# Value products of the attention stage: turned for the local heads, one per head instead of one per map for the differential heads

## The chip, the cores and the metric

One NeuronCore of a Trainium2 chip runs the whole kernel. Its engines are TensorE (PE; PEld is its weight load), VectorE (DVE), ScalarE (ACT), GpSimd (POOL) and SyncE (SP). The metric is the time of one execution on the device, in microseconds; the rows below come from one profiled execution.

## The reference

Two transformer blocks run on 256 tokens of width 1024, all in f32. The change lies in the attention of the second block, between its input projection and its output projection. This is what is computed there:

```python
# 8 local heads (SWA) on 2 key/value heads: window of 128, a sink, 64 wide
scores = einsum("bnqhgd,bnkhd->bnhgqk", qb, kk) * HEAD_DIM ** -0.5 - slope * dist   # masked
p = softmax(concatenate([scores, sink], axis=-1))[..., :-1]
out = einsum("bnhgqk,bnkhd->bnqhgd", p, vv)          # then rms_norm over all 512 columns
# 4 differential heads: two maps each, one value head of 128
p = softmax(s)                                       # s: (b, h, 2 maps, q, k), causal
p_diff = p[:, :, 0] - lam * p[:, :, 1]
out = einsum("bhqk,bkhe->bqhe", p_diff, v)           # then rms_norm over each head's 128
```

Both outputs side by side, 1024 columns, are multiplied with `w_out`.

## The kernel before, in words

Activations lie feature by token (128 features on the partitions, 256 tokens along the row). A large product is made three times in f32r, high and low parts of weight and activation (`products`, L1852 to L1854). Weights stream through a ring of four units: ScalarE rounds a unit to `w_hi`, VectorE (in this stage) makes `w_lo`, three units ahead of use.

The second block's input projection `in2` has 18 units, its output projection `out2` 8. The attention is threaded between them in numbered steps, one unit per step in steps 0 to 17, written out by hand in `make_steps`; each engine has one loop over `STEPS` and does in each step, in a fixed order, what the step's entries say. An engine takes its instructions in order, so one that waits holds up all behind it. Nothing is planned at run time.

There are 16 maps of softmax scores (`MAPS`): 0 to 7 are the local heads, 8 to 15 the two maps of each differential head. Map m goes through these steps:

- step m+3 (a pair of maps at once, every second step): TensorE's `score_pair` (L2125), four f32 products on halves of the array, 64 rows each; VectorE's `biased_max` (L1627, L1634): bias and mask, then two maxima; ScalarE's `exps` (L1063) with row sums.
- step m+4: TensorE's `transposes` (L2145) of the three 128x128 pieces of probabilities into `probT_ps`; ScalarE's `copy_prob_T` (L1071); VectorE's `denominators` (L1640, L1645).
- step m+5: TensorE's `value_product` (L2160 to L2163), three f32 products with the transposed probabilities as weights and V as the moving operand (64 columns wide for a local head, 128 for a differential one) into `pv_ps`; VectorE's `scaled_output` (L1654, L1661, L1665) divides by the denominators and adds the second map to the first.

When all local heads (i = 0) or both maps of a differential head (i = 1 to 4) are there, ScalarE squares and sums (`y_squares`, L1080), VectorE makes the mean square (`y_mean_square`, L1670), GpSimd raises it to -1/2 (L714), VectorE scales (`y_scaled`, L1677). TensorE transposes 128 columns of the result, a chunk (`y_transposes`, L2178); VectorE applies the gain (`y_gained`, L1688, L1691), ScalarE rounds (`round_chunk`, L817), VectorE makes the rest (`rest_of_chunk`, L1234). There are 8 chunks, 0 to 3 local, 4 to 7 differential, and `out2` multiplies each with 8 units of weights.

Step 18 and later have no projection unit; there `out2_part(i, first, end)` begins unit i with the chunks that are there. One step, LATE_STEP, does its chunk after the scores and not before; up to it `y_scaled` stands behind `biased_max` on VectorE, and from it on ahead. VectorE's order in a step is: mean square, copies out of the projection (`copy_out`, L1613), gains, denominators, scaled output, (late scaling), rests of chunks, bias and maxima, (scaling), `w_lo` (L1168).

Of the kernel before, what the change touches and what calls it, by code (L numbers as in the profile page):

```python
# [20 lines left out]
P = 128  # L21
# [65 lines left out]
N_MAPS, N_SWA = 16, 8  # L87

# [7 lines left out]
LATE_STEP = 16  # L96
# [5 lines left out]
def make_steps():  # L102
    steps = [dict(unit=u if u < len(IN2_TILES) else None, copies=[], v_trans=None, pair=None,
                  score=None, trans=None, pv=None, y_sum=None, y_scale=None, y_chunks=[], out2=None)
             for u in range(23)]
# [9 lines left out]
    for i in range(5):  # L115
        at = (7 if i == 0 else 7 + 2 * i) + 5
        steps[at]["y_sum"], steps[at + 1]["y_scale"] = i, i
        steps[at + 2]["y_chunks"] = [0, 1] if i == 0 else [3 + i]
        if i == 0:
            steps[at + 3]["y_chunks"] = [2, 3]  # L120
    there = 0
    for n, step in enumerate(steps):
        if 0 <= n - len(IN2_TILES) < OUT2_BEGUN:
            step["out2"] = (n - len(IN2_TILES), there)
        there += len(step["y_chunks"])
# [6 lines left out]
for _step in STEPS:  # L132
# [4 lines left out]
    _tiles += _y_tiles + _v_tiles  # L137
# [102 lines left out]
def tile_release():  # L240
# [21 lines left out]
    for tile, t in IN2_TILE.items():  # L262
        r[t] = ("src_ready", CHUNK0["y"] + tile[1] + (2 if tile[1] < 4 else 1)) if tile[0] == "y" else \
            ("v_ready", tile[1] + 1) if tile[0] == "v_T" else ("copied", COPIED[tile])
# [6 lines left out]
def build(nc, d):  # L271
# [4 lines left out]
    with ExitStack() as ctx:  # L276
# [102 lines left out]
        y_a, y_b = place("y_a", [P, 2, 512]), place("y_b", [P, 2, 512])  # L379
# [14 lines left out]
        def y_tile(c):  # L394
# [4 lines left out]
            return bank[IN2_TILE["y", c - half] % RING][:, half * TOK:(half + 1) * TOK]  # L399

# [111 lines left out]
        yT_done = sem("yT_done")  # L512
        post_gain_in = sem("post_gain_in")
# [98 lines left out]
        def _(pool):  # L612
# [80 lines left out]
            for c in range(DC):  # L693
# [5 lines left out]
                if c > 0:  # L699
# [9 lines left out]
                                    ).then_inc(rstd_ready, 1)  # L709
            for n, step in enumerate(STEPS):  # L710
                if step["y_scale"] is not None:
                    i = step["y_scale"]
                    pool.wait_ge(y_ms_done, i + 1)
                    nc.gpsimd.tensor_tensor(y_rstd[:, i, :], y_ms[:, i, :], minus_half[:, 0:2],  # L714
                                            ALU.pow).then_inc(y_rstd_done, 1)
                if 0 < n <= len(IN2_TILES):
                    rest_of_unit(UNIT0["in2"] + n + LEAD)
# [45 lines left out]
        def _(act):  # L763
# [309 lines left out]

            def y_squares(i):
                act.wait_ge(y_done, 2 * (8 if i == 0 else 8 + 2 * i))
                for b in range(2):
                    part = y_a[:, b, :] if i == 0 else y_b[:, b, P * (i - 1):P * i]
                    if 2 * i + b:
                        act.wait_ge(y_ss_done, 2 * i + b)
# [4 lines left out]
            for n, step in enumerate(STEPS):  # L1084
                for c in step["y_chunks"] if n != LATE_STEP else []:
# [7 lines left out]
                if step["v_trans"] is not None:  # L1093
                    copy_v(step["v_trans"])
                if step["trans"] is not None:
                    copy_prob_T(step["trans"])
                if 3 <= n < len(IN2_TILES) + len(OUT2_SIDE):
# [30 lines left out]
            act.wait_ge(y_ss_done, 10)  # L1128
# [31 lines left out]
        def _(dve):  # L1160
# [476 lines left out]
            def denominators(m):  # L1637
                kind, h, part = MAPS[m]
                dve.wait_ge(exp_done, 2 * (m + 1))
                nc.vector.reciprocal(rden[:, m, :], row_sum[:, m, :]).then_inc(den_done, 1)  # L1640
# [7 lines left out]
            def scaled_output(m):  # L1648
                kind, h, part = MAPS[m]
                dve.wait_ge(pv_done, m + 1)  # L1650
                dve.wait_ge(den_done, DEN[m])
                for b in range(2):
                    if kind == "swa":
                        nc.vector.tensor_scalar(y_a[:, b, HD * h:HD * (h + 1)],  # L1654
                                                pv_ps[:, HD * b:HD * (b + 1)],
                                                rden[:, m, b:b + 1], None, ALU.mult
                                                ).then_inc(y_done, 1)
                    else:
                        y, pv = y_b[:, b, P * h:P * (h + 1)], pv_ps[:, P * b:P * (b + 1)]
                        if part == 0:  # L1660
                            nc.vector.tensor_scalar(y, pv, rden[:, m, b:b + 1], None, ALU.mult  # L1661
                                                    ).then_inc(y_done, 1)
                        else:
                            dve.wait_ge(y_done, 2 * m)
                            nc.vector.scalar_tensor_tensor(y, pv, rden[:, m, b:b + 1], y, ALU.mult,  # L1665
                                                           ALU.add).then_inc(y_done, 1)

            def y_mean_square(i):
                dve.wait_ge(y_ss_done, 2 * (i + 1))
                nc.vector.tensor_scalar(y_ms[:, i, :], y_ss[:, i, :], 1.0 / (512 if i == 0 else P),  # L1670
                                        EPS, ALU.mult, ALU.add).then_inc(y_ms_done, 1)

            def y_scaled(i):
                dve.wait_ge(y_rstd_done, i + 1)
                for b in range(2):
                    y = y_a[:, b, :] if i == 0 else y_b[:, b, P * (i - 1):P * i]
                    nc.vector.tensor_scalar(y, y, y_rstd[:, i, b:b + 1], None, ALU.mult  # L1677
                                            ).then_inc(y_norm, 1)

            def y_gained(c):  # L1680
# [3 lines left out]
                dve.wait_ge(yT_done, (c // 2 * 2 + 2) if c < 4 else c + 1)  # L1684
                src_free(n)
                source = y_tile(c)
                if c < 4:
# [720 lines left out]
```

## Time and profile before

| | us |
|---|---|
| median of 3 runs | 759.88 (759.86 to 760.01) |
| profiled execution | 760.85 |
| its span, first to last instruction | 758.9 |
| PE busy | 749.4 (99%) |
| PEld busy | 728.1 (96%) |
| DVE busy | 581.2 (77%) |
| ACT busy | 447.7 (59%) |
| POOL busy | 211.6 (28%) |

A row of a timeline begins with its start, counted from the span's start, and its length; "x3" means three records merged into one row; a bracket at its end tells how long the engine sat idle before it and what ended that.

### The profile page before, as it was taken

The numbers are of one execution on the slowest core, as the hardware profiler recorded it, in microseconds if no ns is written. First come the engines' busy times: TensorE is split into PE (matmuls) and PEld (weight loads), VectorE is DVE, ScalarE is ACT, GpSimd is POOL, SyncE is SP. The second block draws the span as 40 slices with busy tenths as digits, with TensorE's granted clock in tenths as the row PEclk, the third lists the DMA queues.
The fourth block names the chain that finished last, engine by engine and source line by source line (L and its number), as shares of the span: only waits on it lengthen the run. The fifth ranks groups of instructions, "written<-read, shape, count | busy, mean of one in ns | idle before, by whom it ended". The sixth has DMA issues, their size and how long they took to land.

```text
span 758.9 us, 16885 instructions
## 1 busy us (share of the span) xinstructions
PE 749.4 (99%) x5994; PEld 728.1 (96%) x5994; DVE 581.2 (77%) x1071; ACT 447.7 (59%) x751; POOL 211.6 (28%) x138
## 2 busy tenths in 40 slices
PE   9999999999999999999999999999999999999997
PEld 8999999999999999999999989999999999988885
DVE  5898986768888877435977896799999999973333
ACT  6644455466665665445855666877666666643431
POOL 0477643460000000342563002522122122122220
PEclk9999999999999999999999999999999999999999
DMA  8565554555555567545443333455555555665651
GB/s 293 191 224 193 184 164 134 195 187 200 188 193 187 177 222 250 189 141 187 141 167 111 114 111 112 139 176 198 196 184 189 193 187 180 214 221 189 183 183 55
DMA packets 37919, 135.49 MB, mean 179 GB/s; under 512 B 4465, under 2 KB 4721, under 8 KB 37873
## 3 DMA queue, kind: packets, MB, share of 16 engines
q1 hardware_dynamic: 37728, 134.86, 53.3%
q8 instruction: 31, 0.51, 0.3%
q14 instruction: 16, 0.12, 0.1%
q10 hardware_dynamic: 144, 0.00, 0.0%
HBM read 133.80 MB, written 1.05 MB: 178 GB/s over the span
## 4 chain that ended last, share of the span: by engine, by line
PE 85%; DVE 5%; ACT 4%; issue 3%; POOL 2%; DMA 1%; DVEq 0%; SPq 0%; POOLq 0%; ACTq 0%
PE bank L1852 24%; PE bank L1853 23%; PE bank L1854 23%; PE bank L2295 4%; PE bank L2294 4%; PE bank L2293 4%; DVE w_lo L1168 2%; ACT w_hi L773 2%; POOL X L741 1%; DMA X<-in_x 1%; PE bank L1908 1%; PE bank L2125 1%; PE bank L2145 0%; ACT score L1063 0%; POOL w_lo L622 0%
## 5 line engine op out<-in xcount | busy, mean ns | idle before, releaser
L1852 PE MATMUL bank<-h_hi,w_hi 128*128 128x256 f32 x1372 | 386.1, 281 | 1.1 <-DVE h_lo L1180 1.0
L1853 PE MATMUL bank<-h_lo,w_hi 128*128 128x256 f32 x1372 | 383.0, 279 | 0.0
L1854 PE MATMUL bank<-h_hi,w_lo 128*128 128x256 f32 x1372 | 383.0, 279 | 0.0
L773 ACT ACTIVATE w_hi<-raw 128x1024 fp32r<-128x1024 f32 (+2 forms) x243 | 258.8, 1067 | 89.9 <-PE bank L2295 41.0
L1168 DVE TENSOR_TENSOR w_lo<-raw,w_hi 128x1024 fp32r<-128x1024 f32 (+2 forms) x187 | 236.1, 1264 | 94.3 <-ACT w_hi L773 92.3
L1852 PEld LDWEIGHTS bank<-h_hi,w_hi 128*128 128x128 f32 x1372 | 257.9, 188 | 2.7 <-DVE w_lo L1246 0.8
L1853 PEld LDWEIGHTS bank<-h_lo,w_hi 128*128 128x128 f32 x1372 | 257.9, 188 | 0.0
L1854 PEld LDWEIGHTS bank<-h_hi,w_lo 128*128 128x128 f32 x1372 | 257.8, 188 | 0.0
L622 POOL TENSOR_TENSOR w_lo<-raw,w_hi 128x1024 fp32r<-128x1024 f32 (+1 forms) x56 | 139.0, 2484 | 380.8 <-ACT w_hi L773 372.6
L1226 DVE TENSOR_TENSOR bank<-bank,scales 128x256 f32<-128x256 f32 x116 | 49.5, 430 | 26.2 <-PE bank L1854 17.6
L1507 DVE SCALAR_TENSOR_TENSOR cg<-bank,vec,cg 128x255 f32<-128x255 f32 x108 | 51.3, 475 | 0.7 <-ACT cg L1003 0.6
L635 POOL TENSOR_TENSOR sumsq<-sq,sumsq 128x256 f32<-128x256 f32 x34 | 35.0, 1037 | 56.5 <-ACT sq L797 56.0
L2293 PE MATMUL bank<-w_hi,f_hi 128*128 128x512 f32 x128 | 49.9, 390 | 0.0
L2295 PE MATMUL bank<-w_lo,f_hi 128*128 128x512 f32 x128 | 49.9, 390 | 0.0
L2294 PE MATMUL bank<-w_hi,f_lo 128*128 128x512 f32 x128 | 49.9, 390 | 0.0
L1852 PE MATMUL bank<-f_hi,w_hi 128*128 128x256 f32 x176 | 49.1, 279 | 0.0
L1853 PE MATMUL bank<-f_lo,w_hi 128*128 128x256 f32 x176 | 49.1, 279 | 0.0
L1854 PE MATMUL bank<-f_hi,w_lo 128*128 128x256 f32 x176 | 49.1, 279 | 0.0
L1282 DVE SCALAR_TENSOR_TENSOR conv<-bank,vec,conv 128x256 f32<-128x256 f32 x120 | 48.4, 475 | 0.0
L1497 DVE TENSOR_TENSOR f_lo<-src,f_hi 128x256 f32 (+1 forms) x54 | 42.8, 793 | 0.5 <-ACT f_hi L954 0.5
L954 ACT ACTIVATE f_hi<-src 128x256 f32 (+1 forms) x54 | 22.2, 411 | 31.3 <-DVE src L1525 31.3
L1003 ACT ACTIVATE cv<-bank,vec 128x256 f32<-128x256 f32 x32 | 18.1, 564 | 38.1 <-DVE bank L1226 38.1
(232 smaller groups left out, 978.8 us busy)
## 6 DMA issues: line engine op xcount, KB each, us to landing
raw<-in_w_up SPq DMA_DIRECT2D x108, 512.0 KB, 3.3
raw<-in_w_in SPq DMA_DIRECT2D x53, 512.0 KB, 3.5
raw<-in_w_down SPq DMA_DIRECT2D x32, 512.0 KB, 4.1
raw<-in_w_down SPq DMA_DIRECT2D x16, 704.0 KB, 4.1
raw<-in_w_o SPq DMA_DIRECT2D x8, 512.0 KB, 3.3
raw<-in_w_gate SPq DMA_DIRECT2D x8, 512.0 KB, 3.4
raw<-in_w_out SPq DMA_DIRECT2D x8, 512.0 KB, 3.3
raw<-in_w_b_out SPq DMA_DIRECT2D x4, 512.0 KB, 3.7
```

What stands on the lines that cost most here:

```text
L622: nc.gpsimd.tensor_tensor(w_lo[s][:, cols], raw[s][:, cols], w_hi[s][:, cols].bitcast(f32), ALU.subtract).then_inc(lo_ready[s], 1)
L773: nc.scalar.activation(hi_of(u)[:, cols], raw[s][:, cols], ACT.Copy).then_inc(hi_ready, 1)
L1168: nc.vector.tensor_tensor(lo_of(u)[:, cols], raw[s][:, cols], hi_of(u)[:, cols].bitcast(f32), ALU.subtract).then_inc(lo_ready[s], 1)
L1226: nc.vector.tensor_tensor(tile, tile, scales[:, 0, :], ALU.mult).then_inc(scaled, 1)
L1282: nc.vector.scalar_tensor_tensor(conv[:, i, :], a_pad[i][:, tap:tap + TOK], w, conv[:, i, :], ALU.mult, ALU.add).then_inc(conv_step, 1)
L1507: nc.vector.scalar_tensor_tensor(c[:, k:TOK], source[:, 0:TOK - k], vcol(w, 3 * col + (2 - k)), c[:, k:TOK], ALU.mult, ALU.add).then_inc(t ...
L1852: nc.tensor.matmul(ps, wh, hi[:, k, :], start=start and n == 0, stop=False)
L1853: nc.tensor.matmul(ps, wh, lo[:, k, :], start=False, stop=False)
L1854: last = nc.tensor.matmul(ps, wl, hi[:, k, :], start=False, stop=stop and n == len(ks) - 1)
L2293: nc.tensor.matmul(to, f_hi[:, k, tok], wh, start=start, stop=False)
L2294: nc.tensor.matmul(to, f_lo[:, k, tok], wh, start=False, stop=False)
L2295: return nc.tensor.matmul(to, f_hi[:, k, tok], wl, start=False, stop=stop)
```

## The change

Local heads: two maps (one of each key/value head) are multiplied in one turned group, `swa_value_products`: V is the weight (64 columns for each head), the transposed probabilities move, and the output lies feature by token, the two heads on the two halves of the partitions. The denominators are spread over 64 columns, transposed on TensorE into the other half of `pv_ps`, copied out by ScalarE (`keep_denominators`) and multiplied in by VectorE (`keep_swa`). The squares are summed by ScalarE, GpSimd and TensorE, and the root is spread over the partitions by two transposes (`broadcast_swa_rms`); the four transposes of two `y_a` blocks go, as the output needs none. The rows of `w_out` and the gain are reordered on the host to suit.

Differential heads: GpSimd multiplies the first map's probabilities with its reciprocals (`scale_first`), VectorE adds the second map to it (`join`), and only the joined map is transposed, copied and multiplied. Scaling and squares read `pv_ps` directly. Everything behind the join comes one step later; there are 24 steps instead of 23, and LATE_STEP is 17 instead of 16.

```diff
     for m in range(N_MAPS):
-        steps[m + 3]["score"], steps[m + 4]["trans"], steps[m + 5]["pv"] = m, m, m
+        steps[m + 3]["score"], steps[m + 4]["den"] = m, m
+        if m < N_SWA:
+            steps[m + 4]["trans"] = m
+        if m < N_SWA and m % 2 == 1:
+            steps[m + 5]["swa_pv"] = m // 2
+        if m >= N_SWA and m % 2 == 1:
+            h = (m - N_SWA) // 2
+            steps[m + 5]["trans"], steps[m + 6]["pv"] = N_SWA + h, h
...
+    steps[13]["swa_stat"], steps[14]["swa_rms"] = True, True
+    steps[15]["swa_chunks"], steps[16]["swa_chunks"] = [0, 1], [2, 3]
+    for i in range(1, 5):
+        at = 13 + 2 * i
         steps[at]["y_sum"], steps[at + 1]["y_scale"] = i, i
-        steps[at + 2]["y_chunks"] = [0, 1] if i == 0 else [3 + i]
+        steps[at + 2]["y_chunks"] = [3 + i]
...
+            def scale_first(m):                                    # GpSimd
+                pool.wait_ge(den_done, DEN[m])
+                for b, (lo, hi) in enumerate(block_cols(m)):
+                    nc.gpsimd.tensor_scalar(score[:, m % N_SWA, lo:hi], score[:, m % N_SWA, lo:hi],
+                                            rden[:, m, b:b + 1], None, ALU.mult
+                                            ).then_inc(first_scaled, 1)
...
+            def join(m):                                           # VectorE
+                dve.wait_ge(den_done, DEN[m])
+                dve.wait_ge(first_scaled, m - N_SWA + 1)
+                for b, (lo, hi) in enumerate(block_cols(m)):
+                    second = score[:, m % N_SWA, lo:hi]
+                    nc.vector.scalar_tensor_tensor(second, second, rden[:, m, b:b + 1],
+                                                   score[:, (m - 1) % N_SWA, lo:hi], ALU.mult, ALU.add
+                                                   ).then_inc(diff_joined, 1)
+            def keep_swa(p):
+                dve.wait_ge(den_kept, p + 1)
+                nc.vector.tensor_tensor(y_a[:, p, :], pv_ps[:, 0:TOK], swa_den[p % 2][:], ALU.mult
+                                        ).then_inc(y_done, 4)
+            def swa_source(c):
...
+                nc.vector.scalar_tensor_tensor(src[n % 2][:], y_a[:, c, :], vcol("swa_out_g_2", c),
+                                               swa_scales[:], ALU.mult, ALU.mult).then_inc(src_ready, 1)
...
+            def swa_value_products(p):                             # TensorE
+                pe.wait_ge(v_ready, 1)
+                pe.wait_ge(probT_done, 2 * p + 2)
...
+                for b in range(2):
+                    nc.tensor.transpose(pv_ps[:, TOK + b * P:TOK + (b + 1) * P], rden_swa[p % 2][:, b * P:(b + 1) * P],
+                                        ident[:])
+                rows = [slice(HD * g, HD * g + HD) for g in range(2)]
+                for g in range(2):
+                    nc.tensor.matmul(pv_ps[rows[g], 0:TOK], v_a[:, 0, rows[g]], prob_T[g][:, 0:TOK],
+                                     start=True, stop=False)
+                for g in range(2):
+                    nc.tensor.matmul(pv_ps[rows[g], P:TOK], v_a[:, 1, rows[g]],
+                                     prob_T[g][:, 2 * P:3 * P], start=False, stop=True
+                                     ).then_inc(pv_done, 1)
+            def swa_mean_squares():
...
+                pe.wait_ge(swa_sum_step, N_SWA // 2 - 1)
+            def broadcast_swa_rms():
...
+                pe.wait_ge(y_rstd_done, 1)
+            def value_product(h):
...
+                pe.wait_ge(probT_done, N_SWA + h + 1)
+                if h:
+                    pe.wait_ge(y_norm, 2 * h)
...
             for n, step in enumerate(STEPS):                       # VectorE's loop
...
                 for tile, unit in step["copies"]:
                     copy_out(tile, unit)
+                if step["swa_rms"]:
+                    swa_mean_square()
+                for c in step["swa_chunks"]:
+                    swa_source(c)
...
+                if step["den"] is not None:
+                    denominators(step["den"])
+                if step["den"] is not None and step["den"] >= N_SWA and step["den"] % 2 == 1:
+                    join(step["den"])
+                if step["swa_pv"] is not None:
+                    keep_swa(step["swa_pv"])
...
             for n, step in enumerate(STEPS):                       # TensorE's loop
...
+                if n == len(STEPS) - 2:
+                    for i in (0, 1):
+                        out2_part(i, BEGUN_WITH[i], DC - 1)
                 if n == len(STEPS) - 1:
-                    out2_part(0, BEGUN_WITH[0], DC - 1)
+                    for i in range(2, OUT2_BEGUN):
+                        out2_part(i, BEGUN_WITH[i], DC - 1)
```

## Rows read from the trace of the kernel before

**Rows 1.** Busy us in a window: length, PE, PEld, DVE, ACT, POOL, clock, DMA.

```profile
425.95:478.97 53.02, 52.10 (x438) 49.91 (x437) 39.88 (x101) 37.15 (x97) 9.07 (x11) 1.00 0.36 120
```

**Rows 2.** Timeline of PE, steps 4 to 6: start, length, instruction.

```profile
392.29 0.37 PE L1852 MATMUL bank<-h_hi,w_hi 128*128 128x256 f32 x1
...
395.18 0.33 PE L2160 MATMUL bank<-v_a,prob_T 128*128 128x64 f32 x2
...
395.80 0.50 PE L2145 MATMUL bank<-ident,score 128*128 128x128 f32 x3
396.22 0.92 PE L2125 MATMUL bank<-kT_a,qT_a 64*128 64x128 f32 x8
397.08 0.38 PE L1852 MATMUL bank<-h_hi,w_hi 128*128 128x256 f32 x1
397.30 0.28 PE L1853 MATMUL bank<-h_lo,w_hi 128*128 128x256 f32 x1
```

**Rows 3.** Timeline of PE, step 15.

```profile
439.01 0.60 PE L2178 MATMUL bank<-ident,y_a 128*128 128x128 f32 x4
439.45 0.39 PE L2160 MATMUL bank<-v_b,prob_T 128*128 128x128 f32 x2
...
440.12 0.49 PE L2145 MATMUL bank<-ident,score 128*128 128x128 f32 x3
```

**Rows 4.** Timeline of PE, first and last of five late waits.

```profile
444.97 0.38 PE L2111 MATMUL bank<-ident,v_T 128*128 128x128 f32 x2
445.48 0.55 PE L2145 MATMUL bank<-ident,score 128*128 128x128 f32 x3
...
464.68 0.28 PE L1854 MATMUL bank<-y_hi,w_lo 128*128 128x256 f32 x1
464.97 0.41 PE L2178 MATMUL bank<-ident,y_b 128*128 128x128 f32 x2
```

**Rows 5.** Timeline of DVE, step 15.

```profile
440.45 0.17 DVE L1670 TENSOR_SCALAR y_ms<-y_ss 128x2 f32<-128x2 f32 x1 [0.66 <-ACT cg L1080]
440.57 0.42 DVE L1613 SCALAR_TENSOR_TENSOR v_T<-bank,scales 128x256 f32<-128x256 f32 x1
440.91 0.87 DVE L1688 TENSOR_SCALAR src<-bank,vec 128x256 f32<-128x256 f32 x2
441.70 0.16 DVE L1640 RECIPROCAL rden<-row_sum 128x2 f32<-128x2 f32 x1
...
442.02 0.61 DVE L1661 TENSOR_SCALAR y_b<-bank,rden 128x128 f32<-128x128 f32 x2
442.54 0.75 DVE L1234 TENSOR_TENSOR y_lo<-src,y_hi 128x256 fp32r<-128x256 f32 x2
443.21 0.55 DVE L1627 SCALAR_TENSOR_TENSOR score<-dist,bank 128x384 f32<-128x384 f32 x1
443.80 0.61 DVE L1634 TENSOR_REDUCE neg_max<-score 128x1 f32<-128x128 f32 x2
444.32 0.47 DVE L1677 TENSOR_SCALAR y_b<-y_b,y_rstd 128x128 f32<-128x128 f32 x2
444.71 1.22 DVE L1168 TENSOR_TENSOR w_lo<-raw,w_hi 128x1024 fp32r<-128x1024 f32 x1
```

**Rows 6.** Timeline of DVE: the copy out of the projection that ends at 395.18.

```profile
395.38 0.42 DVE L1613 SCALAR_TENSOR_TENSOR qT_a<-bank,scales 128x256 f32<-128x256 f32 x1
```

**Rows 7.** Timeline of ACT: exponentials, squares, and a rounding.

```profile
438.70 0.41 ACT L1063 ACTIVATE score<-score,neg_max 128x128 f32<-128x128 f32 x1 [0.61 <-DVE neg_max L1634]
...
439.60 0.30 ACT L1080 ACTIVATE cg<-y_b 128x128 f32<-128x128 f32 x1
...
448.88 0.40 ACT L817 ACTIVATE y_hi<-src 128x256 fp32r<-128x256 f32 x1
```

**Rows 8.** GpSimd: timeline of one power; one line's count, ns min/median/max.

```profile
440.70 0.70 POOL L714 TENSOR_TENSOR y_rstd<-y_ms,minus_half 128x2 f32<-128x2 f32 x1 [8.92 <-DVE y_ms L1670]
...
L725 POOL TENSOR_SCALAR X<-X,vec x8: 917/924/1890, 387.3 to 401.8; 128x256 f32<-128x256 f32 x8
```

More of the change, by code:

```diff
@@ L87 @@
 N_MAPS, N_SWA = 16, 8
+N_DIFF = (N_MAPS - N_SWA) // 2
+N_PROB = N_SWA + N_DIFF
 PIECE = P + 2
@@ L95 @@
 LATE_Y = 5
-LATE_STEP = 16
+LATE_STEP = 17
 OUT2_BEGUN = 4
@@ L103, in make_steps @@
     steps = [dict(unit=u if u < len(IN2_TILES) else None, copies=[], v_trans=None, pair=None,
-                  score=None, trans=None, pv=None, y_sum=None, y_scale=None, y_chunks=[], out2=None)
-             for u in range(23)]
+                  score=None, trans=None, pv=None, y_sum=None, y_scale=None, y_chunks=[], out2=None,
+                  den=None, swa_pv=None, swa_stat=False, swa_rms=False, swa_chunks=[])
+             for u in range(24)]
     for u, tile in enumerate(IN2_TILES):
@@ L124, in make_steps @@
             step["out2"] = (n - len(IN2_TILES), there)
-        there += len(step["y_chunks"])
+        there += len(step["y_chunks"]) + len(step["swa_chunks"])
     return steps
@@ L715, in _ @@
                                             ALU.pow).then_inc(y_rstd_done, 1)
+                if step["den"] is not None and step["den"] >= N_SWA and step["den"] % 2 == 0:
+                    scale_first(step["den"])
                 if 0 < n <= len(IN2_TILES):
@@ L1084, in _ @@
             for n, step in enumerate(STEPS):
-                for c in step["y_chunks"] if n != LATE_STEP else []:
+                if n and STEPS[n - 1]["swa_rms"]:
+                    act.wait_ge(swa_rms_done, 1)
+                    nc.scalar.activation(swa_scales[:], bank[slot(IN2_TILE["swa_rms", 0])][:, 0:TOK],
+                                         ACT.Copy).then_inc(swa_scaled, 1)
+                for c in step["swa_chunks"] + (step["y_chunks"] if n != LATE_STEP else []):
                     round_chunk(CHUNK0["y"] + c, y_hi[:, c, :])
@@ new lines, in swa_mean_squares @@
+            def swa_mean_squares():
+                t = IN2_TILE["swa_stat", 0]
+                bank_free(t)
+                pe.wait_ge(swa_sum_step, N_SWA // 2 - 1)
+                for b in range(2):
+                    last = nc.tensor.matmul(bank[slot(t)][:, b:b + 1], swa_sum[:, b * P:(b + 1) * P],
+                                            ones_over[:, P:P + 1], start=True, stop=True)
+                last.then_inc(swa_stat_done, 1)
+            def broadcast_swa_rms():
+                t = IN2_TILE["swa_rms", 0]
+                bank_free(t)
+                pe.wait_ge(y_rstd_done, 1)
+                for b in range(2):
+                    last = nc.tensor.transpose(bank[slot(t)][:, b * P:(b + 1) * P],
+                                               y_rstd[:, 0, b:b + 1].broadcast_to([P, P]), ident[:])
+                last.then_inc(swa_rms_done, 1)
@@ new lines, in value_product @@
+            def value_product(h):
+                cols = slice(P * h, P * (h + 1))
+                pe.wait_ge(v_ready, h + 2)
+                pe.wait_ge(probT_done, N_SWA + h + 1)
+                if h:
+                    pe.wait_ge(y_norm, 2 * h)
+                else:
+                    pe.wait_ge(y_done, 2 * N_SWA)
+                pt, v = prob_T[h % 2], v_b
+                nc.tensor.matmul(pv_ps[:, 0:P], pt[:, 0:P], v[:, 0, cols], start=True, stop=True)
+                nc.tensor.matmul(pv_ps[:, P:2 * P], pt[:, P:2 * P], v[:, 0, cols],
@@ L2210, in _ @@
                         y_transposes(c)
+                if step["swa_pv"] is not None:
+                    swa_value_products(step["swa_pv"])
                 if step["pv"] is not None:
@@ L2218, in _ @@
                     score_pair(step["pair"])
+                if step["swa_stat"]:
+                    swa_mean_squares()
+                if step["swa_rms"]:
+                    broadcast_swa_rms()
                 if n == LATE_STEP:
@@ L2221, in _ @@
                         y_transposes(c)
-            for i in range(1, OUT2_BEGUN):
-                if BEGUN_WITH[i] < DC - 1:
-                    out2_part(i, BEGUN_WITH[i], DC - 1)
             out2_part(OUT2_SIDE[0], 0, DC - 1)
```

152 lines of the change are left out of this document (79 added, 73 removed).

## The prediction

> **What bounds the kernel now.** The first view is the busy time by windows over the stretch that the change touches, from the end of step 12's projection to the last product of `out2`: of 53.02 us TensorE is busy 52.10, at a granted clock of 1.00 (its 2.4 GHz level), VectorE 39.88, ScalarE 37.15, GpSimd 9.07 [rows 1]. TensorE works its list in order and almost never stops, so a change pays here what it takes out of that list and what waits it leaves in it. The second view is TensorE's timeline. There the price of a group is the distance from its start to the next group's start, since the records overlap [rows 2, 3]. The third is the same timeline in the late steps, read for distances that are too long: transposes at 445.48 start 0.51 after a pair that takes 0.22 (0.29 of waiting), those at 464.97 start 0.29 after a product that takes 0.12 (0.17). There are five such places from the one to the other, 1.7 us together [rows 4]. The fourth is what they wait for: the timelines of VectorE, ScalarE and GpSimd in one late step [rows 5 to 8]. Behind one wait of 0.66 for the squares, VectorE's instructions follow on each other there with no gap. It is nearly the bound of steps 14 to 18 already, which the 39.88 of the whole stretch hides.
>
> **The change on TensorE alone.** Removed: 8 triples of 64-wide products at 0.62 (395.18 to 395.80) [rows 2], 4.9; 8 transposes of `y_a` at 0.11 (four take 0.44), 0.9; 4 triples of transposes at 0.33, 1.3; 4 triples of 128-wide products at 0.67 (439.45 to 440.12), 2.7 [rows 3]. Together 9.8. Added: 8 transposes of denominators, 0.9; 2 that spread the mean square, 0.2; 2 products for that mean square, f32, taken at the 0.22 of a 128-wide one, 0.45; four turned groups.
>
> A turned group has no row. The nearest is the score pair: also four f32 products, two over 128 columns and two over 256, also on halves of the array, there halves by rows. It takes 0.86 (396.22 to 397.08), and the change of shape costs 0.09 before it (0.42 for three transposes that take 0.33) and 0.1 behind it, where the first product of the next group takes 0.22 instead of 0.12 [rows 2]. I take that row, 1.07, so 4.3 for four. Bounds: without any cost of the changes of shape 0.65 (1.7 less in all); with no overlap of the halves 2 x 0.45 + 2 x 0.22 at the pitch of [rows 3], plus the changes, 1.65 (2.3 more). Added in all 5.85, so TensorE's list gets 4.0 shorter (1.7 to 5.7).
>
> **The waits.** Prices of the other engines, start to start: copy out of a projection 0.34, y source of a diff chunk 0.40, reciprocal and its product with lambda 0.32, rest of a chunk 0.33, bias 0.59, the two reductions 0.52 (0.61 to their end), w_lo 1.2 [rows 5]; a copy starts 0.20 after its projection ends [rows 2, 6]; exponentials 0.90, two squares with their sums 0.85, a rounding 0.4 [rows 7]; the power 0.70, begun 0.25 behind its mean square [rows 5, 8]. New ones: an SWA source reads like a copy, 0.35 (bounds 0.2 to 0.45); the join 0.26 (half of the 0.52 of two 128-wide products) plus 0.34, 0.60 (0.3 to 0.9); the scaling that now reads PSUM 0.52 like those two, where 0.39 stood. Projection 2.85, chunk product in `out2` 0.36 [rows 2].
>
> (a) Step 14. TensorE transposes (0.33) and then must spread the SWA root, `broadcast_swa_rms`. Its mean square stands on VectorE behind the copy of step 14's own projection: 0.20 + 0.34 + 0.25 + 0.70 + 0.05, 1.55 after the projection's end. TensorE waits 1.2; behind it stand the whole next projection and all that follows.
>
> (b) Step 17. `value_product(1)` must wait for `y_scaled(1)`, since both use `pv_ps`, and `y_scaled(1)` is last but one in VectorE's step 16 (16 is before LATE_STEP). From the end of projection 15, VectorE: 0.20, copy 0.34, two SWA sources 0.70, reciprocals 0.32, join 0.60, two rests 0.67: bias(12) at 2.83. Exponentials at 4.06, squares of head 0 at 4.96, mean square at 5.8. Then in step 16 copy, two sources, reciprocal, two rests, bias and reductions, 3.1: `y_scaled` at 8.9, done at 9.5. TensorE has until then 0.67 + 1.07 + 2.85 + 0.22 + 0.33 + 2.85, 8.0. Wait 1.6 (the join's and sources' bounds make it 0 to 2.7).
>
> (c) Step 18. `out2_part(0, 0, 5)` needs chunk 4, which is made in step 17, LATE_STEP, behind the score pair. Before, a whole projection lay between. Counted from `value_product(1)`: VectorE has w_lo, copy, reciprocals and join and is at bias(14) by 2.25; exponentials from 3.5 to 4.4; rounding to 4.85. TensorE needs it at 0.67 + 1.07 + 0.22 + 4 x 0.36, 3.4. Wait 1.45, and 0.35 more for the rest of the chunk: 1.8.
>
> (d) Step 20, chunk 5. From there TensorE has 5.2 of work; VectorE has w_lo, mean square, the wait for the power, scaling 0.52, bias and reductions 1.1, w_lo, source 0.48, so the rounding ends at 5.7, and the rest of the chunk, behind reciprocals and join, at 6.5. Wait 1.1.
>
> (e) Steps 21 to 23. Squares, w_lo, mean square, power, scaling end 4.3 after the last value product starts; TensorE has 3.3 of work, so the last transposes wait 1.0. The same chain one head earlier, and chunk 6, add 0.8. Together 1.8.
>
> The local heads up to step 12 leave no wait worth a row: the turned group's copy, product and square end before the next projection does. DMA is not touched: no transfer is added, and VectorE's w_lo stays two projections ahead of use. The square's sum moves to GpSimd, which is idle there. Sum: -4.0 on the list, -1.7 for the old waits, +7.5 for the new, +1.8. The profiled execution took 760.85 (span 758.9 and 1.95 around it), so 762.7; the median of the runs is 0.97 lower, 759.88, and I forecast 761.7.
>
> **A rule against the change.** While VectorE worked, GpSimd's scaling of 128x256 took 0.92 in the median and 1.89 at most [rows 8]. Taken so, `scale_first` is 1.4 for its two halves, 2.8 at worst, with a step of about 4.5 to hide in. The Trainium skill (SBUF — State Buffer, section "SBUF: two separate sides") says that GpSimd and a VectorE instruction with two SBUF inputs lock one port pair for a whole instruction, and the other blocks. By that rule `scale_first(12)` would also hold up step 16's rests and lengthen (b) by up to 0.9, for 762.6; rows 8 agree that someone is held up, but show GpSimd.
>
> **Rivals.** First, the halves by columns don't overlap. For it: the trace has halves by rows only, and these take their moving data from different partitions, while two column halves both need all 128. Against it: the order of the four products alternates the halves as the pair does. Price 2.3: 764.0. The Trainium skill (TensorE: Matmul & The Clock Gate, Part 3, "The mechanism") says that weight loads overlap running products only where the row group differs, which here it does not; no row of this trace shows it.
>
> Second, on the other side: VectorE is quick enough. Place: steps 15 to 17. If joins, sources and scalings take half their price, `y_scaled(1)` is done 8.0 after projection 15, and (b) and (c) never arise: 3.4 less, -1.6, 758.3. The chain of (b) must lose 1.6 of its 9.5 for that; the sign turns at 1.8 saved in all. For it: in the stretch VectorE has 13 us to spare [rows 1]. Against it: in the late step it has none [rows 5].
>
> Third, GpSimd is late: at 3.8 for `scale_first` the joins wait for it, 1.3 more, 763.0. For it the 1.89; against it that the worst doubling gives 2.8.
>
> **How the numbers follow.** Forecast 0.55 (761.7, own range 760.3 to 763.0), no overlap 0.18, quick VectorE 0.17, late GpSimd 0.10. What a measurement can tell from no change is 0.2%, 1.5 us, so 758.4 and 761.4 are the edges. Slower: 0.18 + 0.10 + half of 0.55, 0.56. Faster: the quick VectorE with turned groups at their lower bound, and the forecast's tail, 0.15. Same: the rest, 0.29. Range 759.4 to 764.0: it takes in the first and third rival and half of the second.
>
> **What would show it.** Right: in the changed trace three transposes of step 14 followed by 1.2 us without a product, ended by GpSimd's power; value products of the second head 1 to 2 us late, ended by VectorE; the fifth chunk of the first `out2` part late by more than 1 us; a turned group of about 1 us. Wrong: turned records that start one after another (first rival), VectorE with gaps in steps 15 to 17 (second), joins that wait for GpSimd (third). If TensorE's waits in the stretch stay under 4 us, the forecast's sign is wrong.

## The result, and the profile after

The changed kernel takes 763.38 us in the median of six runs (762.94 to 764.24), the kernel before 760.01 beside it: a ratio of 1.0043, 95% interval 1.0031 to 1.0054. It is slower by 3.4 us; forecast were 1.8. The profiled execution took 762.94, with a span of 760.9.

The medians can be off by an offset that the kernel before has too: some runs of most kernels are about 1.5 us later than the rest, and where a trace shows it, that has arisen before projection 3 begins. So the traces are compared over one stretch, from the start of projection 3's second half (386.24 in the trace before, 384.94 after) to the end of `out2`. Busy time by windows over that stretch, first of the kernel before (length; PE, PEld, DVE, ACT, POOL; clock; DMA share; GB/s), then of the changed kernel, whole and by part:

```profile
386.24:478.97 92.73, 91.66 (x777) 87.85 (x776) 69.88 (x172) 60.79 (x155) 25.56 (x27) 1.00 0.38 127
```
```profile
384.94:480.97 96.03, 88.28 (x731) 81.84 (x730) 72.86 (x150) 61.05 (x156) 35.17 (x38) 1.00 0.36 123
...
424.64:433.18 8.54, 8.54 (x75) 7.75 (x74) 6.78 (x16) 4.83 (x13) 2.96 (x3) 1.00 0.37 124
433.18:441.00 7.82, 6.66 (x57) 6.18 (x56) 5.90 (x18) 4.50 (x12) 3.24 (x3) 1.00 0.40 136
441.00:448.00 7.00, 4.94 (x43) 4.76 (x42) 6.34 (x18) 4.65 (x16) 2.46 (x3) 1.00 0.23 75
448.00:455.00 7.00, 5.13 (x41) 4.67 (x42) 5.55 (x14) 3.94 (x15) 0.36 (x1) 1.00 0.25 75
455.00:462.00 7.00, 5.84 (x50) 5.63 (x49) 5.88 (x14) 4.88 (x14) 2.41 (x4) 1.00 0.44 152
462.00:469.00 7.00, 5.85 (x49) 5.47 (x48) 3.83 (x9) 2.01 (x7) 0.89 (x2) 1.00 0.44 150
```

TensorE is busy 3.4 us less and idle 6.7 us more (7.75 against 1.07), which makes the 3.3 of the stretch. What [rows 1] showed, an engine that almost never stops, ends at step 14. The places stand in TensorE's timeline of the changed kernel (start, length, instruction, and in brackets the idle time and who ended it). The first two lines are a wait that was not foreseen, ahead of the transposes of map 1; then a turned group; then the five places of the prediction, each by the product ahead of the wait and the one behind it:

```profile
393.76 0.28 PE L1926 MATMUL bank<-h_hi,w_lo 128*128 128x256 f32 x1
394.15 0.55 PE L2221 MATMUL bank<-ident,score 128*128 128x128 f32 x3
...
398.40 0.38 PE L2233 MATMUL bank<-ident,tmp 128*128 128x128 f32 x2
398.71 0.65 PE L2237 MATMUL bank<-prob_T,v_a 128*64 128x256 f32 x4
399.19 0.39 PE L2240 MATMUL bank<-prob_T,v_a 128*64 128x128 f32 x4
399.51 0.55 PE L2221 MATMUL bank<-ident,score 128*128 128x128 f32 x3
...
433.18 0.49 PE L2221 MATMUL bank<-ident,score 128*128 128x128 f32 x3
434.83 0.41 PE L2258 MATMUL bank<-ident,y_rstd 128*128 128x128 f32 x2 [1.16 <-POOL y_rstd L749]
...
445.66 0.28 PE L1926 MATMUL bank<-h_hi,w_lo 128*128 128x256 f32 x1
448.01 0.46 PE L2271 MATMUL bank<-v_b,prob_T 128*128 128x128 f32 x2 [2.06 <-DVE y_b L1746]
...
451.26 0.28 PE L1926 MATMUL bank<-y_hi,w_lo 128*128 128x256 f32 x1
453.40 0.38 PE L1924 MATMUL bank<-y_hi,w_hi 128*128 128x256 f32 x1 [1.86 <-DVE y_lo L1290]
...
458.72 0.28 PE L1926 MATMUL bank<-y_hi,w_lo 128*128 128x256 f32 x1
460.16 0.38 PE L1924 MATMUL bank<-y_hi,w_hi 128*128 128x256 f32 x1 [1.16 <-DVE y_lo L1290]
...
464.19 0.28 PE L1926 MATMUL bank<-y_hi,w_lo 128*128 128x256 f32 x1
464.93 0.39 PE L1924 MATMUL bank<-y_hi,w_hi 128*128 128x256 f32 x1 [0.46 <-DVE y_lo L1290]
...
466.69 0.28 PE L1926 MATMUL bank<-y_hi,w_lo 128*128 128x256 f32 x1
467.66 0.41 PE L2289 MATMUL bank<-ident,y_b 128*128 128x128 f32 x2 [0.69 <-DVE y_b L1746]
```

A wait is counted as the distance between two starts less the usual one (0.12 behind a product, 0.33 behind three transposes): (a) 1.32, (b) 2.23, (c) 2.01, (d) 1.32, (e) 0.62 and 0.85. Three more, unforeseen, stand ahead of the transposes of maps 1, 3 and 5: 0.27, 0.19, 0.19. All together 9.0.

The turned group runs 0.48 for four records over 256 columns, 0.32 for four over 128, then 0.10 of change behind it and 0.09 before: 1.0, as priced from the score pair of [rows 2]. One after the other, at the pitch of [rows 3], the two column halves would need 1.3 for the products and not 0.8; the records of the two halves start 0.01 apart. So the column halves run side by side as the row halves do.

VectorE's timeline of the changed kernel: the reciprocal of the local heads, then the steps 15 and 16 that (b) waits for; its answer to [rows 5]:

```profile
391.07 0.94 DVE L1698 RECIPROCAL tmp<-row_sum 128x128 f32<-128x128 f32 x1
...
439.66 0.75 DVE L1715 SCALAR_TENSOR_TENSOR score<-score,rden 128x128 f32<-128x128 f32 x2
440.33 0.76 DVE L1290 TENSOR_TENSOR y_lo<-src,y_hi 128x256 fp32r<-128x256 f32 x2
441.00 0.55 DVE L1683 SCALAR_TENSOR_TENSOR score<-dist,bank 128x384 f32<-128x384 f32 x1
...
443.90 0.17 DVE L1740 TENSOR_SCALAR y_ms<-y_ss 128x2 f32<-128x2 f32 x1 [0.58 <-ACT cg L1128]
443.99 0.42 DVE L1669 SCALAR_TENSOR_TENSOR qT_b<-bank,scales 128x256 f32<-128x256 f32 x1
444.33 0.87 DVE L1735 SCALAR_TENSOR_TENSOR src<-y_a,vec,ev 128x256 f32<-128x256 f32 x2
445.12 0.16 DVE L1701 RECIPROCAL rden<-row_sum 128x2 f32<-128x2 f32 x1
445.30 0.94 DVE L1290 TENSOR_TENSOR y_lo<-src,y_hi 128x256 fp32r<-128x256 f32 x2
446.16 0.54 DVE L1683 SCALAR_TENSOR_TENSOR score<-dist,bank 128x384 f32<-128x384 f32 x1
446.73 0.61 DVE L1690 TENSOR_REDUCE neg_max<-score 128x1 f32<-128x128 f32 x2
447.26 0.60 DVE L1746 TENSOR_SCALAR y_b<-bank,y_rstd 128x128 f32<-128x128 f32 x2
```

From its mean square on (443.90) VectorE has no gap until the head is scaled, 3.9 us later, although GpSimd's power, 0.74 long, is done at 444.90.

### The profile page after: what moved, and what is told of

The parts are those of the page before. It is cut to its first block, busy times and chain, and to the rows that moved or that the text cites. A ratio compares the mean times of both kernels' runs of the same rounds, so it can differ in the third digit from the quotient of the medians.

```text
span 760.9 us, 16763 instructions
## 1 busy us (share of the span) xinstructions
PE 745.1 (98%) x5948; PEld 721.1 (95%) x5948; DVE 584.3 (77%) x1049; ACT 448.2 (59%) x752; POOL 221.2 (29%) x149
## 4 chain that ended last, share of the span: by engine, by line
PE 70%; DVE 6%; ACT 3%; issue 3%; POOL 2%; DVEq 0%; POOLq 0%; ACTq 0%
PE bank L1924 19%; PE bank L1926 18%; PE bank L1925 18%; PE bank L2412 4%; PE bank L2413 4%; PE bank L2411 4%; DVE w_lo L1224 2%; ACT w_hi L810 1%; POOL X L778 1%; PE bank L2197 1%; PE bank L2221 1%; PE bank L1980 0%; POOL w_lo L642 0%; POOL sumsq L655 0%; ACT score L1100 0%
```

## The experiments

Two theories. *One chain*: from step 15 on a single chain through VectorE's list and ScalarE's answers to it decides when each differential head arrives; a wait that is taken away in one place turns up in the next. *Separate waits*: each of (a) to (e) is worth its own length. The prediction summed them as separate. All medians are of five rounds (5 to 12 runs), with the kernel before on the same chip; "stretch" runs to the start of `out2`'s last product (before 92.61, changed 95.91).

| kernel | median us | ratio to before, interval | stretch us |
|---|---|---|---|
| scale_early | 763.18 | 1.0046 [1.0032, 1.0061] | 95.60 |
| mean_early | 762.84 | 1.0039 [1.0027, 1.0052] | 95.33 |
| wlo_gpsimd | 765.53 | 1.0070 [1.0057, 1.0083] | 98.87 |
| recip_narrow | 762.83 | 1.0037 [1.0024, 1.0050] | 95.66 |
| turned_alone | 761.49 | 1.0018 [1.0008, 1.0028] | 94.14 |
| joined_alone | 761.67 | 1.0020 [1.0011, 1.0030] | 94.47 |
| no_scale_first | 763.62 | 1.0044 [1.0031, 1.0057] | 96.32 |
| mean_recip | 763.02 | 1.0030 [1.0019, 1.0041] | 94.22 |
| join_narrow | 762.58 | 1.0033 [1.0021, 1.0044] | 95.12 |
| turned_mended | 760.82 | 1.0010 [1.0001, 1.0018] | 93.54 |
| all_reordered | 759.92 | 1.0001 [0.9992, 1.0010] | 92.66 |
| head_on_scalar | 757.88 | 0.9979 [0.9969, 0.9989] | 90.70 |

**scale_early.** The first differential head is scaled ahead of the rests in step 16:

```
-                if step["y_scale"] is not None and n >= LATE_STEP:
+                if step["y_scale"] is not None and n >= LATE_STEP - 1:
```

> VectorE scales the first differential head in step 16 ahead of the rests and the bias, so the wait of the second head's value products (b, 2.2 us) shrinks to what its own probabilities need, about 0.9. Theory one chain (from step 15 on VectorE's list, with ScalarE's answers, sets when each later product can start; a wait removed from one place moves to the next): (b) falls by 1.3 and the wait for chunk 4 (c, 2.0) grows to 3.2; the time stays at 763.2 to 763.4. Rival separate waits (each wait is worth its own length, as the prediction added them up): (c) stays at 2.0, 1.3 less, 762.1.

TensorE's timeline at (b) and at (c):

```profile
446.03 0.28 PE L1926 MATMUL bank<-h_hi,w_lo 128*128 128x256 f32 x1
446.80 0.46 PE L2271 MATMUL bank<-v_b,prob_T 128*128 128x128 f32 x2 [0.49 <-ACT prob_T L1108]
...
450.06 0.28 PE L1926 MATMUL bank<-y_hi,w_lo 128*128 128x256 f32 x1
453.49 0.58 PE L1924 MATMUL bank<-y_hi,w_hi 128*128 128x256 f32 x1 [3.15 <-DVE y_lo L1290]
```

(b) went from 2.23 to 0.65, (c) from 2.01 to 3.31: of 1.6 removed, 1.3 came back one place later. The median fell by 0.2, as one chain said. (d), 1.32, is gone here too, but a stretch at a lower clock behind (c) took as much (last section).

**mean_early.** The local mean square moves from behind the copy of step 14 to step 13, ahead of w_lo:

```
-                if step["swa_rms"]:
-                    swa_mean_square()
...
+                if step["swa_stat"]:
+                    swa_mean_square()
                 if 3 <= n <= len(IN2_TILES) + 1:
                     ahead(UNIT0["in2"] + n)
```

> The local heads' mean square is formed on VectorE in step 13, ahead of w_lo, and not behind the copy of step 14: the root is there before TensorE asks for it, and wait (a), 1.3 us, goes. Both theories: nothing else takes it over, since every engine's list behind it hangs on projection 14 and starts as much earlier, 1.2 less, 762.2. Rival VectorE is the bound from step 12 on already: projection 14 ends 1.3 earlier but VectorE does not, (b) grows from 2.2 to 3.4, and the time stays at 763.4.

Half of the 1.2 came: 0.54 in the median, 0.58 in the stretch. Wait (a) fell from 1.32 to 0.67 only, since GpSimd's power now runs beside VectorE's w_lo and takes 1.63 (elsewhere 0.73). (b) did not grow (2.26), so the rival falls. The timelines of the two (POOL, then DVE):

```profile
432.79 1.63 POOL L749 TENSOR_TENSOR y_rstd<-y_ms,minus_half 128x2 f32<-128x2 f32 x1 [2.12 <-DVE y_ms L1727]
```
```profile
432.62 1.22 DVE L1224 TENSOR_TENSOR w_lo<-raw,w_hi 128x1024 fp32r<-128x1024 f32 x1
```

**wlo_gpsimd.** Two of VectorE's w_lo go to GpSimd:

```
     if UNIT0["in2"] <= u < UNIT0["up2"] + LEAD:
-        return False
+        return u - UNIT0["in2"] - LEAD in (16, 17)
```

> The two w_lo of steps 16 and 17 (1.2 us each on VectorE) go to GpSimd (about 2.5 each there). Theory one chain: VectorE's list gets shorter between (b) and (d), so (c) falls from 2.0 to 0.8 or less and (d) too; about 1.5 less, 761.9, with (b) as it was. Rival separate waits: (c) and (d) hang on TensorE's shorter list and the roundings, nothing changes, 763.4. Rival contention: GpSimd's subtraction holds VectorE's two-operand instructions up as scale_first does the rests (0.86 instead of 0.67), which takes back 0.2 to 0.8: 762.3 to 763.0.

All three missed: it is 2.15 slower than the changed kernel. GpSimd's timeline, then VectorE's beside it:

```profile
449.04 4.69 POOL L642 TENSOR_TENSOR w_lo<-raw,w_hi 128x1024 fp32r<-128x1024 f32 x2 [0.24 <-ACT w_hi L810]
```
```profile
450.30 1.13 DVE L1706 TENSOR_SCALAR rden<-rden,neg_lam 128x2 f32<-128x2 f32 x1
451.46 2.81 DVE L1715 SCALAR_TENSOR_TENSOR score<-score,rden 128x128 f32<-128x128 f32 x2
```

A multiplication of 128x2 that takes 0.23 elsewhere in the same list took 1.13, the join 2.81 and not 0.75: VectorE stood while GpSimd's two subtractions ran, and the wait before chunk 4 became 4.15. The direction was the third theory's, its size was far off: 3.0 were lost at one multiplication and one join, where 1.2 of w_lo was saved. That is not the whole of it. The stretch grew by 3.0, but when the second head is scaled (at 458.40, in the changed kernel at 455.40, and the stretch begins 1.7 later here) only 1.3 of that has arisen. The other 1.6 came ahead of the third head's scaling, while TensorE ran at its lower clock (the third last number) and VectorE waited 0.68 for its transposes; whether the clock alone cost that was not tested:

```profile
459.00:462.00 3.00, 3.00 (x16) 3.00 (x15) 2.28 (x5) 2.38 (x7) 0.87 (x1) 0.50 0.03 5
```

**recip_narrow.** A reciprocal of 128x2, then a spreading multiplication by 1.0:

```
-                    nc.vector.reciprocal(both[:, :, h // 4, :], row_sum[:, m, :].unsqueeze(2)
-                                         .broadcast_to([P, 2, HD])).then_inc(den_done, 1)
+                    nc.vector.reciprocal(rden[:, m, :], row_sum[:, m, :]).then_inc(den_done, 1)
+                    dve.wait_ge(den_done, DEN[m] - 1)
+                    nc.vector.tensor_scalar(both[:, :, h // 4, :], rden[:, m, :].unsqueeze(2)
+                                            .broadcast_to([P, 2, HD]), 1.0, None, ALU.mult
+                                            ).then_inc(den_done, 1)
```

> The wide reciprocal (128x128, 0.94 us) becomes a reciprocal of 128x2 (0.15) and a multiplication by 1.0 that spreads it (about 0.2), eight times. Theory: the early waits at the transposes of maps 1, 3 and 5 (0.27, 0.19, 0.19) hang on the bias that stands behind the wide reciprocal, and go: 0.4 to 0.65 less, 762.7 to 763.0. Rival: they hang on the turned group's copy, product and square instead: no change, 763.4.

0.55 less in the median, 0.25 in the stretch; the wait ahead of map 1's transposes is gone (the group behind it starts 0.36 earlier), those ahead of maps 3 and 5 are not. The reciprocal was the cause of the first only. For the other two the rival holds: in this kernel's trace VectorE's reductions for map 3 end at 403.23, but ScalarE is only then through the denominators' copy, the probabilities, the square and w_hi, and its exponentials end at 404.40, when TensorE has waited since 404.26.

**turned_alone and joined_alone.** One part of the change each, the other as before; the core of the two, in the order of the steps:

```
-        if m >= N_SWA and m % 2 == 1:
-            h = (m - N_SWA) // 2
-            steps[m + 5]["trans"], steps[m + 6]["pv"] = N_SWA + h, h
+        if m >= N_SWA:
+            steps[m + 4]["trans"], steps[m + 5]["pv"] = m, m
```
```
-        if m < N_SWA and m % 2 == 1:
-            steps[m + 5]["swa_pv"] = m // 2
+        if m < N_SWA:
+            steps[m + 5]["pv_a"] = m
```

In the second the local heads' columns stand in the old order while their gains and output weights stand in the new one; no instruction's time hangs on that.

> One part of the change alone: the turned value products, their denominators and the local heads' statistics as in the changed kernel, the differential heads as before (two triples of transposes and two of products each, 23 steps). By the trace TensorE's list gains almost nothing from this part (removed 4.9 + 0.9; added four groups of 1.0, 0.9 for the denominators, 0.65 for the mean square and its root: 0.25 less), and the early waits (0.65) and a wait for the root (0.5 to 1.3) stay. Theory: this part costs 0.8 to 1.5 against the kernel before, 760.8 to 761.5. Rival: the wait for the root is absorbed by the late waits that the kernel before has anyway (1.7), 760.0 to 760.5.

> The other part alone: local heads as before (64-wide products, transposed y_a), the differential maps joined, transposed and multiplied once, a step later. TensorE's list gets 1.3 + 2.7 = 4.0 less than before. Theory one chain: the late end of the list is set by VectorE and ScalarE, which this part makes longer and a step later, so all of the 4.0 goes into waits, and more: the joined kernel is 1.5 to 2.7 slower than the one before, 761.5 to 762.6. Rival separate waits: (b) 2.2, (c) 2.0, (d) 1.3, (e) 1.5 stay, old waits 1.7 and list 4.0 go: 1.3 slower, 761.3. Rival TensorE's list decides: 758 or less.

Each part alone is slower than before, by 1.4 and 1.6; together that is 3.0 of the 3.4. The turned part came within its first range. The join takes 3.6 of busy time off TensorE's list (88.06 in its stretch, before 91.66; said: 4.0) and still loses, near the numbers of both slower theories, so it excludes only that TensorE's list decides. And 0.95 of its loss is a wait that neither the kernel before nor the changed one has: TensorE waits, at 433.43, for VectorE's scaling of the local heads. So the two parts' losses do not simply add up to the whole.

**no_scale_first.** GpSimd's scaling goes by algebra: the second map is joined with the ratio of the two denominators, and the first denominator goes into the square and into `y_scaled`:

```
-                    scale_first(step["den"])
...
-                nc.vector.tensor_scalar(rden[:, m, :], rden[:, m, :], neg_lam[:, 0:1], None,
-                                        ALU.mult).then_inc(den_done, 1)
+                nc.vector.scalar_tensor_tensor(rden[:, m, :], rden[:, m, :], neg_lam[:, 0:1],
+                                               row_sum[:, m - 1, :], ALU.mult, ALU.mult
+                                               ).then_inc(den_done, 1)
```

> GpSimd's scaling of the first map goes, without any instruction in its place: the second map is joined with the ratio of the two (row sum of the first times minus lambda over that of the second), and the first one's denominator goes into the square's scale on ScalarE and into y_scaled's second factor. Theory contention: GpSimd then never works beside the rests (0.86 for two, alone 0.67) and the join, (b) falls by 0.2 to 0.4 and the time by 0.2 to 0.6, 762.8 to 763.2. Rival GpSimd is late for the joins (the prediction's third): 1.3 less, 762.1. Rival nothing waits for it and nobody is held up: 763.4.

It gained nothing: 763.62. The rests of step 16 went from 0.86 to 0.73, but a square that reads its scale from memory takes 0.35 instead of 0.26, and `y_scaled` with a second factor 0.63 for its pair instead of 0.52, so (b) grew by 0.17. The joins never waited for GpSimd.

**mean_recip.** The edit of recip_narrow, and the mean square one place earlier than in mean_early:

```
+                if step["swa_stat"]:
+                    swa_mean_square()
                 if step["score"] is not None:
                     biased_max(step["score"])
```

> Two edits together: the narrow reciprocal, and the local mean square in step 13 ahead of the bias, so that GpSimd's power runs before w_lo and not beside it (there it took 1.63 and not 0.73, and left 0.67 of wait (a)). Theory: power 0.73 again, (a) goes whole, 1.3, and the early waits with it 0.4: 761.7. Rival: the power's 1.63 comes from elsewhere, 0.6 of (a) stays: 762.3. Rival one chain takes it back at (b): 762.8.

In the trace the 1.7 came: GpSimd's power took 0.72, wait (a) and the one of map 1 are gone (maps 3 and 5 keep theirs), the stretch is 1.69 shorter. The nine times lie in two groups, four from 761.2 to 761.9 and five from 763.0 to 763.9; the trace is of the lower, and what parts the upper from it stays open (the mean granted clocks, 0.997 to 1.0 and 0.996 to 0.998, do not), so the median, 763.02, supports no theory.

**join_narrow.** VectorE joins 8 columns of a block only:

```
-                    second = score[:, m % N_SWA, lo:hi]
+                    second = score[:, m % N_SWA, lo:lo + 8]
```

> The changed kernel, but VectorE joins only 8 columns of each block of the second map (left out: the other columns of the join); every wait, GpSimd's scaling and TensorE's list stay. A pair of joins falls from 0.67 to about 0.25. Theory one chain: the joins of steps 15, 17 and 19 stand on the chain one behind another, each gives its 0.4 back, 1.1 to 1.2 less, 762.2. Rival separate waits: (b) and (c) fall by 0.4 each, 762.6. Rival VectorE has time to spare there: 763.4.

0.80 less, the number of the separate waits. By place: (b), (c) and (d) fell by 0.39, 0.39 and 0.38, as one chain said, but 0.31 came back as a new wait ahead of the transposes of the third head. The sum alone would have misled.

**turned_mended.** The edits of turned_alone and of mean_recip together, no others.

> The turned part alone, with the narrow reciprocal and the local mean square ahead of step 13's bias. Theory: what the turned part costs (1.4) is the wide reciprocal and the late root, not the turned products, whose list is even with the old one (0.25 less): 760.2 to 760.5, within what can be told from the kernel before. Rival: the turned products themselves, their changes of shape and their statistics cost it: 761.2 to 761.5, as turned_alone.

760.82, between the two. The two mistakes explain 0.6 to 0.7 of its 1.4. Of the 0.93 left in the stretch 0.26 has arisen by the end of projection 13, the rest later; it was not taken apart further.

**all_reordered.** The whole change with the narrow reciprocal and four edits of order; beside those of mean_recip:

```
+            fresh = steps[n - 1]["swa_chunks"] + steps[n - 1]["y_chunks"]
+            step["out2"] = (n - len(IN2_TILES), there - len(fresh))
...
+                    ahead(UNIT0["in2"] + n)
                     for c in step["y_chunks"]:
                         rest_of_chunk(CHUNK0["y"] + c, y_hi[:, c, :], y_lo[:, c, :])
...
-                if step["y_scale"] is not None and n >= LATE_STEP:
+                if step["y_scale"] is not None and n >= LATE_STEP + 2:
```

> The whole change with orders mended: narrow reciprocal; local mean square ahead of step 13's bias; in step 17 w_lo goes into the gap in which VectorE waits for ScalarE's rounding of chunk 4 (0.96 us); y_scaled of step 18 behind the bias; each out2 part begins only with chunks that are a step old. Theory one chain: VectorE's chain loses 0.8 to 1.6 against mean_recip, whose profiled stretch was 1.7 shorter than the changed kernel's: 759.9 to 760.9, even with the kernel before. Rival: the chain is ScalarE's and GpSimd's answers (squares, power), which no order of VectorE shortens: 761.5, as mean_recip's profiled run.

759.92: even with the kernel before. The five edits together were worth 3.5 us; they were not taken apart. Chunk 4's wait is gone, as the first `out2` part begins without that chunk; in this kernel and the next, (c) stands for the wait ahead of the second head's transposes.

**head_on_scalar.** all_reordered, with squares ahead of the exponentials and the scaling on ScalarE:

```
+                if step["y_scale"] is not None:
+                    y_scaled(step["y_scale"])
+                if step["y_sum"] is not None:
+                    y_squares(step["y_sum"])
                 if step["score"] is not None:
                     exps(step["score"])
```

> all_reordered with the chain of a differential head taken off VectorE's order: ScalarE forms the squares ahead of the exponentials (before, behind them), and ScalarE, not VectorE, scales the head out of PSUM (two copies with a scale, ahead of the exponentials). VectorE loses 0.52 per head, each mean square comes about 0.9 earlier, and y_scaled no longer stands behind rests, bias and reductions. Theory one chain: (b), 2.38 in all_reordered, and (c), 1.75, fall by 1.5 or more together, 758.2 to 759.0, less than the kernel before (759.9). Rival ScalarE becomes the bound: its exponentials come 0.85 later where the squares stand ahead, the joins and so the transposes wait for them, 759.9 to 761.5. Rival VectorE's sources, joins and w_lo alone set the end: 759.9, as all_reordered.

757.88, 2.0 less than all_reordered and 0.21% less than the kernel before: this version beats both. Windows over the stretch, TensorE's timeline at (b), and VectorE's mean square, each first in all_reordered, then here:

```profile
385.04:477.82 92.78, 87.96 (x732) 81.78 (x730) 69.10 (x158) 60.58 (x156) 34.06 (x38) 1.00 0.37 127
384.99:475.82 90.83, 87.66 (x732) 81.72 (x731) 66.79 (x150) 62.86 (x164) 34.76 (x38) 1.00 0.39 130
```
```profile
446.42 0.46 PE L2276 MATMUL bank<-v_b,prob_T 128*128 128x128 f32 x2 [2.10 <-DVE y_b L1750]
445.60 0.46 PE L2273 MATMUL bank<-v_b,prob_T 128*128 128x128 f32 x2 [1.32 <-ACT y_b L1126]
```
```profile
442.31 0.17 DVE L1744 TENSOR_SCALAR y_ms<-y_ss 128x2 f32<-128x2 f32 x1 [0.58 <-ACT cg L1129]
441.62 0.16 DVE L1752 TENSOR_SCALAR y_ms<-y_ss 128x2 f32<-128x2 f32 x1
```

TensorE is idle 3.17 of the stretch (all_reordered 4.82, changed kernel 7.75). The mean square comes at 441.62 and no longer waits for the squares (442.31), and the second head's products come at 445.60 (446.42); (b) is 1.48, (c) 1.06. All_reordered's two waits, 2.38 and 1.75 in the expectation, are 2.26 and 1.63 by this count. Together they fell by 1.35, a little less than the 1.5 of one chain; (d) gave 0.31 more, and the time fell below that theory's range. The two edits were not tried one by one. ScalarE did not become the bound: it is busy 62.86 of 90.83.

## Why the prediction was right, and where it was off

- **TensorE's list, -4.0.** Right. The waits are 9.0 after and 1.7 before, the stretch is 3.3 longer, so the list lost 4.0. The turned group was priced at 1.07 and took 1.0, and the first rival (no overlap of column halves) falls. The Trainium skill's rule on weight loads (TensorE: Matmul & The Clock Gate, Part 3, "The mechanism"), as the prediction read it, would have made the group 1.65; the trace does not agree.
- **(a), 1.2:** 1.32, by the path described; mean_recip takes it away whole.
- **(b), 1.6:** 2.23. TensorE reached it 7.9 after projection 15 (said: 8.0). On VectorE's side each term was a little small: bias(12) at 3.13 (2.83), the mean square at 6.03 (5.8), `y_scaled` at 9.39 (8.9).
- **(c), 1.8; (d), 1.1; (e), 1.8:** 2.01, 1.32, 1.47. The mechanisms stand. That they were added up as separate waits did not hurt the sum, since each was counted on from the wait before it; it would have misled anyone who mends one of them (scale_early).
- **"The local heads up to step 12 leave no wait worth a row":** this step failed. It gave the wide reciprocal no price: at 0.94 it stands ahead of the bias, and 0.27 to 0.36 hang on it (recip_narrow). And it let the turned group's copy, product and square end in time without asking what stands behind them on ScalarE: w_hi and the exponentials of the next odd map, two waits of 0.19.
- **Second rival, a quick VectorE:** falls. The join was priced right (0.60, measured 0.67), and VectorE has no gap between 443.90 and 447.8.
- **Third rival, GpSimd late for the joins:** falls; no join waits for it, and no_scale_first gains nothing.
- **The rule against the change.** Rows first: wlo_gpsimd's 1.13 for 0.23, mean_early's 1.63 for 0.73. The Trainium skill (SBUF — State Buffer, "SBUF: two separate sides") says that one engine holds the shared ports for a whole instruction, and the other blocks; both rows agree, one in each direction. The rests in (b) do not: beside GpSimd's two scalings (0.82 and 0.92 long) they took 0.43 and 0.54, and neither waited for a scaling to end. The price there was up to 0.9; the rests lost 0.13 to 0.19.

The forecast was 1.7 low: 0.65 in the early steps, 0.6 in (b), 0.5 in (a), (c) and (d), less 0.3 in (e), is 1.5 of it. So 763.38 lies beyond the forecast's own range, which ended at 763.0. That it lies in the whole range is partly luck: the room above was left for the first rival, which falls. By the time alone the third rival (763.0) and the first (764.0) came nearer than the forecast; only the trace tells them from it.

## What to carry to other kernels

Take work off the busiest engine's list only after asking which chain feeds it at the end. Here 4.0 us of products went, and the late waits took more back, 7.0 at (b) to (e) against 1.7 before, because links in the chain of a head (squares, mean square, power, scaling) stood behind unrelated work on VectorE and ScalarE. Shorten that chain first: the same products cost 3.4 us more than the kernel before or 1.8 less, by the order of the work around them, one narrower reciprocal and the engine that scales. When a wait is removed, look at the next one down the list before counting the gain.

## What the hardware showed that was not expected

- A VectorE reciprocal of 128x128 took 0.94, one of 128x2 0.15; in recip_narrow a multiplication that writes the same 128x128 took 0.23.
- GpSimd's 128x1024 subtraction stops even a 128x2 multiplication on VectorE until it ends (1.13 instead of 0.23).
- TensorE's clock fell behind some of the long waits and not behind others, and the length of the wait did not decide it. Windows of 3 us behind (c): of the changed kernel (1.86 without a product before it), of mean_early (1.85) and of scale_early (3.15). The third last number is the granted clock; 0.53 is near the lower level, 1.2 of 2.4 GHz:

```profile
453.00:456.00 3.00, 2.60 (x22) 2.60 (x23) 2.22 (x7) 2.22 (x7) 1.36 (x3) 1.00 0.12 29
```
```profile
453.00:456.00 3.00, 2.87 (x16) 2.87 (x17) 2.22 (x7) 2.09 (x5) 1.62 (x3) 0.66 0.21 41
```
```profile
453.00:456.00 3.00, 2.51 (x11) 2.51 (x12) 2.21 (x6) 1.38 (x7) 1.26 (x2) 0.53 0.16 26
```

In scale_early and mean_early the slow stretch cost little: it lies ahead of (d), 1.32, which is gone there, since TensorE arrives later at a chunk that VectorE sets. The same holds for recip_narrow. In no_scale_first and mean_recip the clock fell behind (b), and (c) shrank to 0.64 and 0.46. So a wait that is shorter in such a trace need not be a gain.
